# Attention values against high and low halves side by side, their sum moved to VectorE, and one weight split moved past the projection's copies

## The reference

```
z = h @ w_in                      # pool | q1 q2 | k1 k2 | v | gates
q, k = rope_partial(q), rope_partial(k)
s = einsum('bqhmd,bkhmd->bhmqk', q, k) * ATTN_SCALE
s = where(mask, s, -inf)
p = softmax(s, axis=-1)
a = p[:, :, 0] - lam * p[:, :, 1]
attn = einsum('bhqk,bkhv->bqhv', a, v)
attn = rms_norm(attn, subln_g) * (1 - lam_init)      # per head
```

## Time and profile before

| | |
|---|---|
| median of 3 runs | 952.3 us (951.32 to 953.8) |
| profiled execution | 952.17 us, of which the trace's span is 950.3 us |
| PE, DVE, ACT busy, share of the span | 89%, 65%, 53% |
| stages, us from the span's start | projections, pooling and head 0 up to the first transposed probabilities 0 to 165; heads to 387; gate blocks with the last attention 387 to 455; merge and output projection to 620; experts to 907 |
| one head of the loop | 34.05 us |

### The profile page before, as it was taken

The page is one execution under the profiler, slowest core; times in us unless marked ns, Lnnn a source line. Parts: engine busy times, 40 slices in busy tenths (PEclk is TensorE's granted clock), DMA queues, the critical chain, the costliest instruction groups (busy, mean ns, idle before and its releaser), DMA issues.

```text
span 950.3 us, 15615 instructions
## 1 busy us (share of the span) xinstructions
PE 849.2 (89%) x5052; PEld 749.3 (79%) x5052; DVE 616.4 (65%) x1053; ACT 506.3 (53%) x910; POOL 69.3 (7%) x81
## 2 busy tenths in 40 slices
PE   4998999999999999989898996399999999999930
PEld 4998999888889888879897885377877777777730
DVE  6264224676676767476455223589899899989957
ACT  6224214455554454454623211277888788788844
POOL 0000000000000000000000000111112112112202
PEclk9999999999999999999999997599999999999975
DMA  8622133033023123150423806379999999999534
GB/s 245 151 89 74 42 89 95 1 97 95 20 76 95 41 60 96 37 162 5 133 90 117 304 35 233 119 254 359 358 362 350 362 360 363 366 354 361 196 105 190
DMA packets 154355, 164.97 MB, mean 174 GB/s; under 512 B 19645, under 2 KB 139069, under 8 KB 153770
## 3 DMA queue, kind: packets, MB, share of 16 engines
q1 hardware_dynamic: 148506, 152.68, 48.7%
q0 software_dynamic: 5520, 11.15, 3.1%
q10 hardware_dynamic: 288, 0.59, 0.2%
HBM read 155.93 MB, written 17.36 MB: 182 GB/s over the span
## 4 chain that ended last, share of the span: by engine, by line
PE 80%; DVE 9%; ACT 5%; DMA 3%; issue 3%; ACTq 0%; POOL 0%; POOLq 0%; DVEq 0%; SPq 0%
PE ps L1356 25%; PE ps L1358 23%; PE ps L1357 23%; PE ps L1495 2%; ACT E L744 2%; PE ps L1664 2%; PE ps L1504 1%; PE ps L1617 1%; DVE wl L939 1%; PE ps L1476 1%; ACT wh L708 1%; PE ps L1684 1%; DMA gb<-in_norm_mix_g 1%; DMA xg<-h_rows,idn 1%; DVE x L1335 1%
## 5 line engine op out<-in xcount | busy, mean ns | idle before, releaser
L1285 DVE TENSOR_TENSOR wl<-rawM,wh 128x1024 fp32r<-128x1024 f32 x192 | 227.6, 1222 | 21.1 <-ACT wh L857 19.7
L857 ACT ACTIVATE wh<-rawM 128x1024 fp32r<-128x1024 f32 x195 | 200.1, 1055 | 10.9 <-PE ps L1358 10.1
L1356 PE MATMUL ps<-hTh,wh 128*128 128x272 f32 x448 | 132.1, 295 | 8.1 <-ACT plh L696 3.0
L1358 PE MATMUL ps<-hTh,wl 128*128 128x272 f32 x448 | 130.7, 292 | 0.0
L1357 PE MATMUL ps<-hTl,wh 128*128 128x272 f32 x448 | 129.8, 290 | 0.0
L1356 PE MATMUL ps<-wh,hTh 128*128 128x384 f32 x320 | 116.3, 363 | 8.4 <-ACT qkv L721 6.8
L1356 PE MATMUL ps<-wh,xh 128*128 128x512 f32 x256 | 105.1, 411 | 3.4 <-DVE xl L1308 2.5
L1358 PE MATMUL ps<-wh,hTl 128*128 128x384 f32 x320 | 108.0, 337 | 0.0
L1357 PE MATMUL ps<-wl,hTh 128*128 128x384 f32 x320 | 107.8, 337 | 0.0
L1357 PE MATMUL ps<-wl,xh 128*128 128x512 f32 x256 | 102.0, 398 | 0.0
L1358 PE MATMUL ps<-wh,xl 128*128 128x512 f32 x256 | 101.9, 398 | 0.0
(11 more groups left out here) (255 smaller groups left out, 1599.1 us busy)
## 6 DMA issues: line engine op xcount, KB each, us to landing
rawM<-in_w_expert_gate SPq DMA_DIRECT2D x131, 256.0 KB, 5.2
rawM<-in_w_expert_up SPq DMA_DIRECT2D x131, 256.0 KB, 7.5
rawM<-in_w_expert_down SPq DMA_DIRECT2D x64, 512.0 KB, 8.0
rawA<-in_w_in SPq DMA_DIRECT2D x64, 192.0 KB, 3.0
rawA<-in_w_in SPq DMA_DIRECT2D x20, 512.0 KB, 5.5
rawA<-in_w_attn_branch SPq DMA_DIRECT2D x8, 512.0 KB, 4.6
rawA<-in_w_out SPq DMA_DIRECT2D x8, 512.0 KB, 4.3
fy<-expert_rows SPq DMA_DIRECT2D x4, 1024.0 KB, 9.0
```

What stands on the lines that cost most here:

```text
L857: nc.scalar.activation(wh[:, c % S, :], rawM[:, slot, :], ACT.Copy).then_inc(m_hi, 1)
L1285: V.tensor_tensor(wl[:, c % S, :], rawM[:, slot, :], wh[:, c % S, :].bitcast(F32), ALU.subtract).then_inc(m_lo, 1)
L1356: T.matmul(out, sh, mh_, start=start, stop=False, **kw)
L1358: return T.matmul(out, sl, mh_, start=False, stop=stop, **kw)
```

## The change

1. `vh` and `vl` become the two halves of one tile `vhl`. `values` does two matmuls for a key block in place of three: `ath` times the 256 columns of `vhl` (high result in columns 0 to 127, low result in 128 to 255 of bank 7), and `atl` times the 128 high columns.
2. DVE adds the halves as it copies them out of PSUM: a `tensor_reduce` over pairs writes `att` and counts `av_ev`. It stands in DVE's step behind the softmax difference and ahead of the next maximum. ACT's copy to `att` is gone.
3. ACT squares `att` (`bsq`) from SBUF, and also squares the clamped `asq` (sum in `ssa`), which DVE did. Both stand at the end of ACT's step, behind the exponentials, and wait for the new semaphore `clamped`, which DVE's clamp counts; the clamp waits for `squared`, which ACT counts, of the tile before.
4. The split `nxt(6)` leaves the end of `attend`. ACT does it in the next `head`, between steps 5 and 6 of the head before; DVE does it behind `rope`, ahead of step 6. The same holds for the chunk `GB0 + 2` ahead of the gate blocks.

```diff
@@ ScalarE, step(g, s)
-                if s >= 2:
-                    act.wait_ge(av_mm, NT * g + s - 1)
-                    nc.scalar.activation(bsq[:], ps[:, 7, 0:P], ACT.Square, scale=BIG_SCALE,
-                                         accum_out=ssb[:, s - 2, bass.ds(g, 1)])
-                    nc.scalar.activation(att[:, s - 2, g, :], ps[:, 7, 0:P], ACT.Copy).then_inc(av_ev, 1)
...
+                if s >= 2:
+                    act.wait_ge(clamped, NT * g + s - 1)
+                    nc.scalar.activation(bsq[:], att[:, s - 2, g, :], ACT.Square, scale=BIG_SCALE,
+                                         accum_out=ssb[:, s - 2, bass.ds(g, 1)])
+                    nc.scalar.activation(asq[:], asq[:], ACT.Square,
+                                         accum_out=ssa[:, s - 2, bass.ds(g, 1)]).then_inc(squared, 1)
@@ ScalarE, attend and head
-                    if s == 4:
-                        nxt(6)
...
-                if not (isinstance(h, int) and h == 1):
+                first = isinstance(h, int) and h == 1
+                if not first:
                     step(h - 2, NT)
+                hi_head(2, n + 2, h)
+                if not first:
                     step(h - 2, NT + 1)
@@ VectorE, step(g, s, lk)
+                if s >= 2:
+                    dve.wait_ge(av_mm, NT * g + s - 1)
+                    V.tensor_reduce(att[:, s - 2, g, :], ps[:, 7, 0:2 * P].rearrange("p (r d) -> p d r", r=2), AX.X,
+                                    ALU.add).then_inc(av_ev, 1)
...
                 if s >= 2:
                     dve.wait_ge(av_ev, NT * g + s - 1)
-                    lk(V.tensor_scalar(asq[:], att[:, s - 2, g, :], CLAMP, -CLAMP, ALU.min, ALU.max))
-                    ins = V.scalar_tensor_tensor(out=asq[:], in0=asq[:], scalar=1.0,
-                                                 in1=asq[:], op0=ALU.mult, op1=ALU.mult,
-                                                 accum_out=ssa[:, s - 2, bass.ds(g, 1)])
-                    lk(ins)
+                    if not (isinstance(g, int) and g == 0 and s == 2):
+                        dve.wait_ge(squared, NT * g + s - 2)
+                    V.tensor_scalar(asq[:], att[:, s - 2, g, :], CLAMP, -CLAMP, ALU.min, ALU.max).then_inc(clamped, 1)
@@ VectorE, head
                 rope(h - 1, lk)
+                lo_head(2, n + 2)
                 if not first:
                     step(h - 2, NT + 1, lk)
@@ TensorE, values(g, t)
-                    ins = three(ps[:, 7, 0:P], ath[:, kb, :], atl[:, kb, :], vh[:, v, :], vl[:, v, :],
-                                kb == 0, kb == len(vs) - 1)
+                    T.matmul(ps[:, 7, 0:2 * P], ath[:, kb, :], vhl[:, v].rearrange("p r d -> p (r d)"),
+                             start=kb == 0, stop=False)
+                    ins = T.matmul(ps[:, 7, 0:P], atl[:, kb, :], vh[:, v, :], start=False, stop=kb == len(vs) - 1)
```

More of the change, by code:

```diff
@@ L171, in build @@
         ktl = hr("ktl", [P, 2 * P], F32R)
-        vh = hr("vh", [P, NT + 1, P], F32R)
-        vl = hr("vl", [P, NT + 1, P], F32R)
+        vhl = hr("vhl", [P, NT + 1, 2, P], F32R)
+        vh, vl = vhl[:, :, 0, :], vhl[:, :, 1, :]
         ath = hr("ath", [P, 4, P], F32R)
@@ L269, in build @@
                              "ath_done", "atl_done", "av_mm", "av_ev"))
+        clamped, squared = sem("clamped"), sem("squared")
         an_done, at_mm, at_hi, at_lo = sem("an_done"), sem("at_mm"), sem("at_hi"), sem("at_lo")
@@ L783, in gate_block @@
                                      ps[:, 2 * (b % 2):2 * (b % 2) + 2, 0:HALF], ACT.Copy).then_inc(gb_ev, 1)
-            split_to(H0 + 6)
+            split_to(H0 + 5)
             act.wait_ge(out_done, 32)
@@ L802, in _ @@
             act.wait_ge(ws_dve, len(dve_jobs))
-            split[0] = GB0 + 3
+            split[0] = GB0 + 2
             step(HEADS - 2, NT)
+            split_to(GB0 + 2)
             gate_block(0)
@@ L807, in _ @@
             gate_block(1)
-            attend(HEADS - 1, lambda k: split_to({3: GB0 + 3, 4: GB0 + 5, 5: GB0 + 7, 6: 0}[k]), GATE_BLOCKS)
+            attend(HEADS - 1, lambda k: split_to({3: GB0 + 3, 4: GB0 + 5, 5: GB0 + 7}[k]), GATE_BLOCKS)
             step(HEADS - 1, NT)
@@ L1046, in lo_head @@
                                 ALU.subtract).then_inc(lo_done, 1)
-            per_head = 1 + 6 * NT
-            per_tail = 6
+            per_head = 1 + 4 * NT
+            per_tail = 2
             def step(g, s, lk):
@@ L1142, in _ @@
             links[0] = d1 + per_head * (HEADS - 2)
-            split[0] = GB0 + 3
+            split[0] = GB0 + 2
             step(HEADS - 2, NT, link)
             rope(HEADS - 1, link)
+            split_to(GB0 + 2)
             step(HEADS - 2, NT + 1, link)
-            attend(HEADS - 1, lambda k: split_to({3: GB0 + 3, 4: GB0 + 5, 5: GB0 + 7, 6: 0}[k]), link)
+            attend(HEADS - 1, lambda k: split_to({3: GB0 + 3, 4: GB0 + 5, 5: GB0 + 7}[k]), link)
             step(HEADS - 1, NT, link)
@@ L1154, in _ @@
             big, one = BIG_SUM / (BIG_SCALE ** -2), 2.0 ** 128 * BIG_SCALE ** 2
+            dve.wait_ge(squared, NT * HEADS)
             link(V.tensor_scalar(fin[:], ssb[:], big, None, ALU.is_ge))
```

## The result

The changed kernel takes **972.28 us** (median of 4 runs, 971.07 to 973.32). The kernel before, run beside it, takes 951.81 us (4 runs, 950.47 to 953.8). The ratio is 1.0215 with a 95% interval of 1.020 to 1.023: slower by 2.15%. The sign is as predicted; the time lies 2.3 us above the top of the range and 8.7 us above the value.

A forecast was written before the change was run, and what follows sets the result against it. It took PE's waits for DVE and ACT at three places a head to decide: 1.79 us a loop head, 10.7 over heads 2 to 7, 0.99 in head 1, -0.3 under the gate blocks; +11.4 on 952.17 gives 963.6 us, range 957 to 970.

The forecast's parts named there:

- The sign: Whole kernel: the change makes it slower, chance 0.87, against 0.08 for faster and 0.05 for same.
- PE's saving: Matmuls of `values`: a key block takes 0.23 us, 0.10 less; 96 blocks, 9.6 us if PE alone decided.
- the wide matmul costs two narrow ones: Rival on PE: a 256-column matmul takes 0.22 us, so a block saves nothing; 968 us, chance 0.04.
- The sum's price: DVE's sum of the halves: 0.42 us, between 0.28 and 0.69, on the chain at 21 places.
- the sum is dear: Rival on DVE: the sum takes 0.6 to 0.7 us because its reads hop; 967 to 969 us, chance 0.18.
- Place 2: At `turn_probs(2)`: two squares on ACT and DVE's sum, less 0.10, cost 0.86 us.
- Place 3 and border: At `turn_probs(3)` 0.21 us more; at the head's border two squares replace the split, a gain of some 0.08.
- Place 1: From the head's start to the first scores: costs 0.80 us, PE's savings of 0.6 us by then notwithstanding.
- The clock: Granted clock expected to stay at 1.00; rival that it falls in the heads: about 10 us more, 975, chance 0.03.

The follow-up runs named there:

- e4: Changed kernel with three 128-column matmuls a key block again, the low half in its own columns: 975.84 us, ratio 1.0237.
- e1: Changed kernel with 12 matmuls of 128 zero columns on PE ahead of a head's first scores: 967.04 us, ratio 1.0147.
- e5: Changed kernel with the two squares of step 2 behind ACT's copy of the weight chunk, not ahead of it: 963.54 us, ratio 1.0104.
- e10: Kernel before with the split moved to where ACT and DVE wait, plus wide pair and sum, squares kept as before: 951.03 us, ratio 0.998.
- e3: Kernel before with only the weight split moved, as the change moves it: 948.27 us, ratio 0.9951.
- e8: Changed kernel with 12 zero matmuls ahead of `turn_probs(2)`, none ahead of the first scores: 971.91 us, ratio 1.0193.
- twice more: Kernel before with the subtraction that makes `vl` done three times on DVE, lengthening the wait before the scores: 966.06 us, ratio 1.0139.
- e9: Kernel before with the subtraction that makes `vl` done four times on DVE, one behind the other: 979.52 us, ratio 1.0273.
- e2: Changed kernel with the weight split back at its old place, at the end of the attention's step 4: 974.24 us, ratio 1.0229.

## Why the prediction was right or wrong

- **PE's saving: right.** A block takes 0.22 to 0.23 us in place of 0.33, as predicted from the earlier trace rows, and e4 shows that the two narrow matmuls would have cost more. The rival "the wide matmul costs two narrow ones" is out. The 134 and 262 cycles of the Trainium skill ("TensorE: Matmul & The Clock Gate", Back-to-back issue gap) would have given the two the same price; the trace doesn't agree, with 0.11 us for 128 columns and 0.12 for 256. They are that section's figures for an isolated matmul, and the prediction left out that for a stream with weight loads the same section gives about 81 ns at 128 columns and 131 ns at 512, by which a wide one is cheaper than two narrow ones, as it was here.
- **The sum's price: right.** 0.419 us, predicted 0.42 from the earlier trace rows. Hopping over 128 columns at each element costs nothing against 425 ns for 256 elements side by side. The rival "the sum is dear" is out. The Trainium skill's 1.73 ns a column ("Vector Engine (DVE) Microarchitecture Reference", 5.2 Measured stream behaviour on trn2) is told there of a two-source program on SBUF, one source of which hops at every element, and does not carry over to this read of PSUM. The prediction missed that the same section has a case nearer to this one: a one-source operation whose stream alternates between two regions at every element and writes one word for two read ran at the full rate. The trace's 0.419 us agrees with that.
- **Place 2: right.** 0.88 us with the clock held (e1), predicted 0.86: two squares and a sum. e5 takes out the squares' part and e10 shows the sum's.
- **Place 3 and border: right in their sum.** 0.15 together, predicted 0.21 - 0.08 = 0.13. That the split's place at the border is taken by the squares is what e3 confirms from the other side: without the squares the wait shrinks by 0.73.
- **Place 1: mis-sized.** 1.00 us where I had 0.80. Two small things: a square that reads SBUF takes 0.31 us, where I took 0.27 from squares that read PSUM, and the moved split waits 0.15 us for ACT's copy (227.89), which I had not drawn. Over six heads this is 1.2 us.
- **The clock: the step that failed.** The prediction says: "The granted clock stayed at 1.00 over the 1.11 us of the border, so I expect 1.00 again." It carried that row over to waits that its own sums made longer, "over 1 us" before the scores and "some 1.4 us" at `turn_probs(2)` (1.48 and 1.44 were measured), so that its sum has no term for the clock. The runs showed a low stretch of 3.4 us in each of heads 2 to 6, at 1.4 us each: 7 us, without which the profiled run would have stood at about 966 us, inside the range. The price was near (an estimate of 10 us more and 975 in all), and the chance of 0.03 was wrong. The longer waits in the trace of before would have warned of it, if not clearly: 1.54, 1.74, 2.13 and 2.81 us had 1.00 behind them, 2.97 us near 90 us had 0.50.

The account closes by the table: 963.6 us, 8.4 more in heads 2 to 6 (7.1 for the low stretches, some 1.2 for place 1 and place 2), 0.2 less in head 7, 0.7 more under the gate blocks and 0.9 behind them are 973.4 us, where the profiled run took 973.32. The 0.7 under the gate blocks are the clock's too as far as is known: in e1, which has no low stretch there, these blocks take 0.7 us less than before, where 0.3 less was predicted.

What stays open is what decides in a single case. A wait of 1.48 us has a fall behind it in five of five loop heads of the changed kernel, in four of e8's, three of e4's and two of e5's; "twice more" had none in its profiled run with 1.42 us and, as inferred, some in its three others; 2.26 us had none in head 2 of e9; and the 2.81 us above have both. Nor do the falls start at a fixed time behind the wait. Wherever heads that follow each other have one, they start 37.55 us apart, in e9 too, where the heads are 37.8 us long, so that there the fall comes 0.7 us behind the end of the wait in head 3 and, three heads on, just ahead of it (346.45 against 346.50). The changed kernel's heads, at 37.55 us with their low stretch, keep that distance, and each of them is hit. No run tests what sets it, nor how often a fall comes at a given length of wait.

## What to carry to other kernels

Price a new wait of the tensor engine twice: for its own length, and, once it comes to some 1.5 us, for what a fall of the clock behind it would cost (here 1.4 us a head); keep that in the range. A trace that shows the clock held over one wait as long is no proof: the kernel before held it over 2.13 and 2.81 us, and the changed one lost it behind 1.48 in each turn of the loop. Work that must go into another engine's queue is better spread so that several short waits come of it than one long one. And a change of two parts should be tried by its parts: here the moved split alone gains 0.4%, and the fold costs 0.3 points of that even with the squares left at their place.

## What the runs showed of the hardware

- The granted clock went to 0.50 (1.2 GHz) for some 3.4 us, near the end of a wait of 1.47 us or more: 1.1 to 1.2 us behind it in the changed kernel's heads, from 0.73 us behind it to 0.05 ahead of it in e9's loop. PE was then mostly working without a gap again. It cost 1.4 us in each head. In the trace of before, waits of 1.11 to 1.23 us at the heads' borders had none, and neither had waits of 1.54, 1.74, 2.13 and 2.81 us in and behind the gate blocks; one of 2.97 us had one.
- In the loop it needs a long wait, not the idle time of a head: e8 took 1.3 us of idle time out at another place and left four of five low stretches where they were, e1 took out the long wait and left none in the loop, and e2 moved them with the longest wait. With waits as long, their number still differed from kernel to kernel (five, four, three and two of five heads).
- The spread of a kernel's own runs goes with the clock: of the 13 runs of the kernel before, that of 951.39 us has a mean clock of 0.959, that of 955.38 us one of 0.952.
- Twelve matmuls of zeros in the wait kept the clock at 1.00 in the loop and gave 5.2 us back (e1).
- A reduction of PSUM in pairs that lie 128 columns apart takes 419 ns (a sum, 128 results a partition), that of as many adjacent elements 425 ns (a maximum, 2 results a partition).
- ACT's square of 128 columns takes 0.31 us from SBUF, and 0.28 us from PSUM.
